# One kernel, three moves: gate products in rows of four, running sums one tile earlier, and a read of x on another queue

## What is computed

```
# block 0: gated linear attention
h = x @ w_in;  q, k, v, z, a = split(h)
g = log_sigmoid(a @ w_a2 + b_a) / 16          # the gates; cumulative sums per chunk of 64
# block 1: indexed sparse attention; after each block: layer norm and a gated side input
# second part: h = rms_norm(x) @ w_in_2, split over five branches
#   A spatial gating, B forgetting attention (big_f = cumsum(log_sigmoid(f))),
#   C mLSTM (b = cumsum(log f); running maximum of i - b), D RWKV-7, M attention to a memory
out = x + concat(branches) * silu(z) @ w_out_2
```

## Time and profile before

| | us |
|---|---|
| median of three runs | 1486.0 (1484.73 to 1486.3) |
| profiled execution, its time | 1486.0 |
| profiled execution, its span | 1484.3 |
| TensorE busy | 1443.8 (97%) |
| VectorE busy | 616.6 (42%) |
| GpSimd busy | 555.9 (37%) |
| ScalarE busy | 526.1 (35%) |

### The profile page before, as it was taken

One profiled execution on the slowest core, in us unless ns is written; L12 is line 12 of the kernel. 1 busy time (PEld: TensorE's weight loads), 2 busy tenths in 40 slices (PEclk: granted clock), 3 DMA queues, 4 the chain that ended last, 5 costly groups with the idle time before them and its releaser, 6 DMA issues.

```text
span 1484.3 us, 25087 instructions
## 1 busy us (share of the span) xinstructions
PE 1443.8 (97%) x10817; PEld 1257.9 (85%) x10817; DVE 616.6 (42%) x1296; ACT 526.1 (35%) x868; POOL 555.9 (37%) x238
## 2 busy tenths in 40 slices
PE   7999999999999999999999999999999999988998
PEld 6888886799999897778788889988997987767897
DVE  6024352123115235379656611344223612487525
ACT  3265223433213332333445521244434322553311
POOL 6333331133332324973374233322434342063221
PEclk9999999999999999999999999999999999998999
DMA  5223321023521323223110043133433222001211
GB/s 175 86 60 99 98 76 39 1 88 104 207 101 58 94 86 113 86 64 107 57 58 30 29 153 115 60 100 114 143 82 95 86 85 86 1 16 59 89 59 57
DMA packets 114668, 122.90 MB, mean 83 GB/s; under 512 B 12665, under 2 KB 107749, under 8 KB 114302
## 3 DMA queue, kind: packets, MB, share of 16 engines
q1 hardware_dynamic: 110864, 113.26, 24.1%
q10 hardware_dynamic: 3694, 8.04, 1.5%
HBM read 114.99 MB, written 6.31 MB: 82 GB/s over the span
## 4 chain that ended last, share of the span: by engine, by line
PE 94%; DVE 2%; ACT 2%; POOL 1%; issue 1%; DMA 0%; SPq 0%; DVEq 0%; ACTq 0%
PE ps L218 89%; PE ps L1462 1%; PE ps L900 1%; PE ps L1468 0%; PE ps L278 0%; ACT xT_high L909 0%; PE ps L3077 0%; PE ps L2278 0%; POOL rk L2814 0%; DMA x_tok<-in_x_dram 0%; DVE xT_low L919 0%; PE ps L2665 0%; PE ps L1038 0%; PE ps L2185 0%; POOL rk L2816 0%
## 5 line engine op out<-in xcount | busy, mean ns | idle before, releaser
L199 POOL TENSOR_TENSOR w_low<-w_ring,w_high 128x2048 fp32r<-128x2048 f32 (+3 forms) x98 | 416.9, 4258 | 707.2 <-ACT w_high L184 671.5
L218 PE MATMUL ps<-w_high,xT_high 128*128 128x256 f32 (+1 forms) x1056 | 303.8, 288 | 6.4 <-POOL w_low L460 4.2
L218 PE MATMUL ps<-w_high,xT_low 128*128 128x256 f32 (+1 forms) x1056 | 296.9, 281 | 0.0
L218 PE MATMUL ps<-w_low,xT_high 128*128 128x256 f32 (+1 forms) x1056 | 296.9, 281 | 0.0
L184 ACT ACTIVATE w_high<-w_ring 128x2048 fp32r<-128x2048 f32 (+1 forms) x91 | 171.5, 1885 | 303.1 <-PE ps L218 302.3
L218 PE MATMUL ps<-xT_high,w_high 128*128 128x512 f32 (+1 forms) x600 | 240.1, 400 | 1.0 <-ACT v_tok L706 0.7
L218 PE MATMUL ps<-xT_high,w_low 128*128 128x512 f32 (+1 forms) x600 | 237.7, 396 | 0.0
L218 PE MATMUL ps<-xT_low,w_high 128*128 128x512 f32 (+1 forms) x600 | 236.7, 394 | 0.0
L218 PEld LDWEIGHTS ps<-w_high,xT_high 128*128 128x128 f32 x1056 | 200.4, 190 | 17.4 <-issue 11.4
L218 PEld LDWEIGHTS ps<-w_low,xT_high 128*128 128x128 f32 x1056 | 200.5, 190 | 2.2 <-issue 2.2
L218 PEld LDWEIGHTS ps<-w_high,xT_low 128*128 128x128 f32 x1056 | 200.3, 190 | 0.0
(11 more groups left out here) (503 smaller groups left out, 2155.9 us busy)
## 6 DMA issues: line engine op xcount, KB each, us to landing
w_ring<-in_gla_w_in_dram SPq DMA_DIRECT2D x24, 1024.0 KB, 5.3
w_ring<-in_dsa_w_in_dram SPq DMA_DIRECT2D x19, 1024.0 KB, 5.2
w_ring<-in_w_in_dram SPq DMA_DIRECT2D x18, 1024.0 KB, 5.2
w_ring<-in_gla_w_out_dram SPq DMA_DIRECT2D x8, 1024.0 KB, 5.1
w_ring<-in_ple_gate_w_dram SPq DMA_DIRECT2D x8, 1024.0 KB, 5.0
w_ring<-in_dsa_w_out_dram SPq DMA_DIRECT2D x8, 1024.0 KB, 4.9
x_scratch<-x SPq DMA_DIRECT2D x4, 1024.0 KB, 6.7
w_ring<-in_w_out_dram SPq DMA_DIRECT2D x4, 768.0 KB, 4.6
```

What stands on the lines that cost most here:

```text
L199: ins = self.nc.gpsimd.tensor_tensor(low[:, part], whole[:, part], high[:, part].bitcast(F32), ALU.subtract)
L218: return self.nc.tensor.matmul(out, lhs, rhs, start=first, stop=last, skip_group_check=not check)
```

## The change

One: the eight gate products of the linear attention are issued in two rows of four, each behind a whole column block (`gates(b)`), instead of one behind each token tile. Two: in the projection the running sums of the log gates are made at one place (behind tile 33) instead of two (behind 33 and 34), and the steps that follow have numbers lower by one; `gates_out` and `mem_turns` keep theirs. Three: the read of x back is issued by SyncE between two of its weight loads instead of by ScalarE behind the U copies, VectorE waits for it ahead of the recurrence instead of ahead of the first addition, and it adds early output tile c in step c instead of in step c + 1.

```diff
--- before.py
+++ after.py
@@ -561,14 +561,14 @@
                         ins = g.split_product(ps[0:GLA_RANK, 4, :], columns(w_a_parts, k), columns(g.xT, k), k == 0, k == KD - 1)
                     ins.then_inc(sem["aT_ready"], add("aT_ready", 1))
 
-                def gate(b, i):
-
-                    if i == 0:
-                        pe.wait_ge(sem["aT_copied"], past["aT_copied"] + 2)
-                    if b:
-                        pe.wait_ge(sem["log_gate"], past["log_gate"] + i + 1)
-                    f = 4 * b + i
-                    g.product(ps[:, 4 + i, :], w_a2[:, f * P:(f + 1) * P], aT[:]).then_inc(sem["u_ready"], add("u_ready", 1))
+                def gates(b):
+
+                    pe.wait_ge(sem["aT_copied"], past["aT_copied"] + 2)
+                    for i in range(4):
+                        if b:
+                            pe.wait_ge(sem["log_gate"], past["log_gate"] + i + 1)
+                        f = 4 * b + i
+                        g.product(ps[:, 4 + i, :], w_a2[:, f * P:(f + 1) * P], aT[:]).then_inc(sem["u_ready"], add("u_ready", 1))
 
                 for c in range(4):
                     for half in range(HALVES):
@@ -593,13 +593,13 @@
                                 ins = g.split_product(ps[:, n % 4, half * CHUNK:(half + 1) * CHUNK], columns(g.xT, k, slice(j * P, (j + 1) * P)),
                                                       columns(w, k), k == 0, k == KD - 1)
                             ins.then_inc(sem[done], add(done, 1))
-                            if c in (1, 2) and half == HALVES - 1:
-                                gate(c - 1, j)
                         g.release(done)
                         if opening:
                             g.turn_tables(pe)
                     if c == 0:
                         low_rank()
+                    elif c < 3:
+                        gates(c - 1)
                 pe.wait_ge(sem["v_copied"], past["v_copied"] + 16)
                 pe.wait_ge(sem["log_gate"], past["log_gate"] + 8)
 
@@ -1849,9 +1849,9 @@
         lg = g.sb(stack, "log_gates", [P, NT, 2 * GH])
         nth_of = {what: nth[i] for i, (_, _, _, _, _, what) in enumerate(tiles)}
         sgu_turns, sgu_masks = 22, 24
-        logs, cums, cum_copies = 30, 33, 35
-        a_turns, a_rows, mu_turns, mu_copies = 36, 37, 38, 39
-        gatings, gate_steps, gated_turns, gates_out = 40, 42, 43, 44
+        logs, cums, cum_copies = 30, 33, 34
+        a_turns, a_rows, mu_turns, mu_copies = 35, 36, 37, 38
+        gatings, gate_steps, gated_turns, gates_out = 39, 41, 42, 44
         mem_turns = 45
         low_tanh = 3 + [what for _, _, _, _, _, what in tiles].index(("small", 0))
         conv_silus = 3 + [what for _, _, _, _, _, what in tiles].index(("kC", 1))
@@ -1907,13 +1907,12 @@
                         for h in range(GH):
                             ins = nc.tensor.transpose(ps[:, 6, h * P:(h + 1) * P], s.w_sgu[:, h, :], g.ident[:])
                         ins.then_inc(sem["w_sgu_turned"], add("w_sgu_turned", 1))
-                    elif i in (cums, cums + 1):
+                    elif i == cums:
                         pe.wait_ge(sem["log_gates"], past["log_gates"] + 1)
-                        for jj in range(NT - 1) if i == cums else (NT - 1,):
+                        for jj in range(NT):
                             for ii in range(jj + 1):
                                 ins = g.product(ps[:, 7, jj * 2 * GH:(jj + 1) * 2 * GH], (g.ones if ii < jj else g.not_before)[:], lg[:, ii, :], ii == 0, ii == jj, check=False)
-                        if i == cums + 1:
-                            ins.then_inc(sem["cum_ready"], add("cum_ready", 1))
+                        ins.then_inc(sem["cum_ready"], add("cum_ready", 1))
                     elif i == a_turns:
                         pe.wait_ge(sem["a_made"], past["a_made"] + 1)
                         for jj in range(NT):
@@ -3300,8 +3299,6 @@
             for j in range(NT):
                 act.wait_ge(sem["U_ready"], past["U_ready"] + j - j % 2 + 2)
                 nc.scalar.activation(U[:, j, :], ps[:, 4 + j // 2, (j % 2) * GW:(j % 2 + 1) * GW], ACT.Copy).then_inc(sem["U_copied"], add("U_copied", 1))
-            act.wait_ge(sem["YT_ready"], past["YT_ready"] + doubled)
-            act.dma_start(x_back, g.x_dram).then_inc(sem["x_back"], add("x_back", 16))
             g.split_high(act, w_out + 3)
 
             def y_squares(j):
@@ -3410,13 +3407,12 @@
             dve.wait_ge(sem["rest_taken"], past["rest_taken"] + 3 * NT)
             for j in range(NT):
                 nc.vector.tensor_tensor(heads(bonus_v[:, j, :]), heads(tok[:, 2, j, :]), bonus[:, j, :].unsqueeze(2).to_broadcast([P, GH, HD]), ALU.mult).then_inc(sem["bonus_v"], add("bonus_v", 1))
+            dve.wait_ge(sem["x_back"], past["x_back"] + 16)
 
             def early_added(u):
 
                 c, j = early_units[u]
                 cols = slice(c * CHUNK, (c + 1) * CHUNK)
-                if u == 0:
-                    dve.wait_ge(sem["x_back"], past["x_back"] + 16)
                 dve.wait_ge(sem["early_ready"], past["early_ready"] + u + 1)
                 nc.vector.tensor_tensor(x_back[:, j, cols], x_back[:, j, cols], ps[:, early_bank(u), 0:CHUNK], ALU.add).then_inc(sem["early_added"], add("early_added", 1))
 
@@ -3437,10 +3433,8 @@
                 for i in range(PAIRS):
                     nc.vector.scalar_tensor_tensor(out=state[:, c + 1, i, :], in0=state[:, c, i, :], scalar=end_decay[:, i, c:c + 1],
                                                                        in1=ps[:, 2 + i, 0:C], op0=ALU.mult, op1=ALU.add).then_inc(sem["state_new"], add("state_new", 1))
-                if c:
-                    early_added(first_early[c - 1])
-
-            early_added(first_early[NCH - 1])
+                early_added(first_early[c])
+
             for j in range(NT):
                 dve.wait_ge(sem["y_sq"], past["y_sq"] + j + 1)
                 sq = y_scratch(j)
@@ -3487,6 +3481,8 @@
         def _(sp):
             sp.wait_ge(sem["mlstm_y_turned"], past["mlstm_y_turned"] + 2)
             g.load_chunks(sp, w_out + RING + 1)
+            sp.wait_ge(sem["YT_ready"], past["YT_ready"] + doubled)
+            sp.dma_start(x_back, g.x_dram).then_inc(sem["x_back"], add("x_back", 16))
             g.load_chunks(sp)
             out_tiles = g.out[0].rearrange("(j p) d -> p j d", p=P)
             for n in range(D // COLS):
```

## The result

The changed kernel takes 1493.55 us (median of 4 runs, 1491.82 to 1495.21), the kernel before 1486.01 us beside it (4 runs, 1484.73 to 1486.3): ratio 1.0053, 95% interval 1.0041 to 1.0065, 7.5 us slower. The prediction said 1485.4 us, in a range of 1483.2 to 1488.5, so the time lies outside the range, on the slow side, to which it gave 0.08. Two executions at a far lower granted clock (one of this kernel, 5005 us, and one of steps_only, 1784 us) are left out of every figure. The profiled execution of the changed kernel took 1492.37 us, with a span of 1490.6 us.

The account below looks back on a forecast made before the run. The prediction took TensorE to bound the kernel, with 94% of the chain. Its terms -2.3 + 1.7 + 0 = -0.6 us gave 1485.4 us from 1486.0, in a range of 1483.2 to 1488.5.

Parts of the forecast that it names:

- What bounds the kernel: Whole kernel: TensorE holds 94% of the chain that ended last, so an edit counts only through TensorE's work or waits.
- First place, the gates (-2.3): Gate products of the linear attention: three of each row of four save 0.39 us of format change, -2.3 us.
- rival A: Gates: each costs 1.25 us also in a row, having its own wait and bank; 1487.7 us, chance 0.10.
- Second place, the steps (+1.7): Running sums and steps one tile earlier: VectorE's scan ends late, TensorE waits 1.7 us for mu_row.
- D: Sums: the scan misses its start before GpSimd's next split, TensorE waits 7.8 us; 1491.5 us, chance 0.04.
- B: Sums: no wait for mu_row, because VectorE is less late than reckoned; 1483.7 us, chance 0.13.
- "0" for the ten products: Running sums: the four products take about 0.82 us behind tile 33 as behind tile 34, so 0.
- Third place, the read of x (0): Read of x on SyncE's queue: lands at 1404.0, just in time for VectorE's recurrence; cost 0, bounds 0 and +3.1 us.
- C: Read of x: the load lands after 1405.4, where the cover ends; 1488.5 us at the chunk rate, chance 0.08.
- VectorE's cover and the additions: Recurrence: TensorE's 1.2 us to spare hides VectorE's wait for the load and additions of 0.33 us per step; 0.
- the list of signs: What the changed profile would show; for the read: SyncE's issue at about 1395.6, landing in under 8 us, no TensorE wait.

Follow-up runs that it names:

- steps_only: Kernel before with only the second part: ten running-sum products at one place and the following steps one tile earlier; 1488.51 us, ratio 1.0017.
- x_act_adds: Kernel before with x read back early on ScalarE's queue, 0.6 us after the last T step, plus VectorE's moved wait and additions; 1485.64 us, ratio 1.0000.
- x_only: Kernel before with only the third part: x read back on SyncE's queue, VectorE's wait and additions moved; 1490.74 us, ratio 1.0035.
- after: The changed kernel, all three parts together, against the kernel before; 1493.55 us, ratio 1.0053.
- gates_only: Kernel before with only the first part: eight gate products in two rows of four; 1487.72 us, ratio 1.0013.
- gate_pairs: Kernel before with the gate products in pairs, behind the second and the fourth token tile; 1485.78 us, ratio 0.9995.
- merge_only: Kernel before with all ten running-sum products behind tile 33, every later step where it stood; 1487.62 us, ratio 1.0009.
- split_sums: Kernel before with the steps one tile earlier but the sums apart, six products behind tile 32, four behind 33; 1490.37 us, ratio 1.0032.
- x_act_same: Kernel before with x read back on ScalarE's queue at the instant SyncE issues it in the changed kernel, VectorE as before; 1490.84 us, ratio 1.0040.
- after_late_read: Changed kernel with SyncE issuing the read of x behind the first WT product, about 1.1 us later; 1490.32 us, ratio 1.0028 against the kernel before.
- pairs_adds: Kernel before with gates in pairs, x read early on ScalarE's queue, and VectorE's additions in their own step; 1485.18 us, ratio 0.9995.

## Why the prediction was wrong, point by point

**What bounds the kernel**: right. Whatever moved the time did so by TensorE.

**First place, the gates (-2.3)**: the saving is right to 0.1 us, rival A is refuted. The sum lacked a term, what the new rows do to TensorE's clock. "What would make the forecast wrong as a whole is a changed pace of TensorE in the stages between, where nothing is edited" came true directly behind the edited places: the rows of four cost +0.7 us in the changed kernel's profile and +1.9 us timed alone.

**Second place, the steps (+1.7)**: VectorE was right throughout, and so was the wait (1.58 us in steps_only); D did not happen (in no profiled execution with the moved steps does a split start before the scan has ended). B looked right in the changed kernel's profile, where no wait is listed, and is not: TensorE came 1.7 us late because of half clock behind the ten products, and so the wait was already paid when it got there. The wait, where it shows, is followed by half clock too. In the changed kernel the place costs 1.7 us, the forecast's size by another way, which is luck; alone it costs +2.7 (3.2 in its rows). "0" for the ten products left out the same term as at the gates: half clock stands behind them in two of four profiled executions, 1.7 us each time. Merged without moving a step they were 1.5 us slower (0.1 to 2.7), which no row shows.

**Third place, the read of x (0)**: here the step failed, "Cost 0". C is refuted, and VectorE's cover and the additions came as worked out (x_act_adds). The load was issued together with the last T step, as the sum had it (not at 1395.6, 0.6 us ahead of it, as the list of signs has it), and took 8.6 us instead of under 8, which the cover of 1.2 us takes up. What I asked was who waits for the load. I did not ask what the load keeps waiting: the 16 KB packets in which TensorE's own instructions arrive over the same DMA engines. One such packet was due 1.6 us behind the very event that now issued the load. It came 3.2 us late, TensorE stood 2.0 us, and half clock followed: 6.8 us of it in the changed kernel's profile (2.9 us of time), 3.4 us in that of x_only. The term is +4.9 us in the changed kernel's rows and +4.9 us timed alone, instead of 0. The rows for it were in the profile before: queue q8 has 85 packets on its page, one of them at 1397.8.

**The sum.** A profiled execution can be followed from place to place by the start of one and the same instruction in it and in the kernel before. The marks are ScalarE's v evictions at 43.2 and 126.30 us (before) for the gates, GpSimd's splits at 1145.1 and 1185.4 us for the sums, and VectorE's last T step at 1396.18 and last state update at 1439.6 us for the read. The table has by how much each kernel gets later between two marks, in us; "elsewhere" is the rest of the difference at the end of the span, from stages that nobody edited.

| kernel | gates | sums | read | elsewhere | together | timed |
|---|---|---|---|---|---|---|
| after | +0.7 | +1.7 | +4.9 | -1.0 | +6.4 | +7.5 |
| gates_only | +1.1 | 0.0 | 0.0 | -0.3 | +0.8 | +1.9 |
| gate_pairs | -1.2 | 0.0 | +0.1 | +1.0 | -0.1 | +0.1 |
| steps_only | 0.0 | +3.2 | 0.0 | +0.1 | +3.3 | +2.7 |
| merge_only | +0.2 | 0.0 | 0.0 | +0.9 | +1.1 | +1.5 |
| split_sums | +0.2 | +3.1 | +0.1 | -1.0 | +2.3 | +4.2 |
| x_only | 0.0 | 0.0 | +3.7 | -0.6 | +3.1 | +4.9 |
| x_act_same | +0.2 | 0.0 | +5.1 | -0.8 | +4.5 | +5.1 |
| after_late_read | +3.0 | +1.6 | +0.1 | +0.3 | +5.0 | +4.2 |
| pairs_adds | -0.8 | 0.0 | +0.1 | +1.6 | +0.9 | -1.0 |

A place that a kernel doesn't touch stays within 0.2 us; the unedited rest moves by 1 us and more from one execution to the next (1.8 us in x_act_adds), so one profile settles where time is lost and not how much in the median. In the changed kernel the forecast's terms -2.3, +1.7 and 0 are +0.7, +1.7 and +4.9: 7.3 us where the sum had -0.6.

The parts timed alone are 1.9 + 2.7 + 4.9 = 9.5 us, the whole 7.5. Half clock behind the sums and the wait for mu_row share the same 1.7 us in the changed kernel, which fits its rows (1.7 us at the sums, 3.2 us in steps_only). But gates and sums together, timed in after_late_read, come to 4.2 us, nearly the 4.6 of the two alone, and most of the missing 2 us would be at the read; the uncertainties are as large, and this was not settled.

**What stays open**: why the clock falls behind one row of gates and not behind the other, and in one execution and not in the next. The Trainium skill (TensorE: Matmul & The Clock Gate, section "What's actually happening") says that the clock follows how busy TensorE has lately been. Behind the wait for mu_row in steps_only and behind the gap at the read, in all three kernels with the gap, the rows agree: TensorE stood, then the clock fell. In split_sums it stood 0.8 and 2.0 us and the clock stayed full. Behind the gates and the sums the rows don't show it: there TensorE's busy time is full in every window before the fall.

## What to carry to other kernels

Before a load is moved, ask not only when it lands and who waits for it, but what else is on the DMA engines in the microseconds behind its issue: the trace lists the packets that bring instructions, and 1 us earlier or later may decide. An engine gap that the profile puts down to "issue" was the sign here. And before small float32 products are gathered into one row, count a half-clock stretch (1.7 us here) against what the row saves: two gates in a row brought none here, four did in some executions.

## What the runs showed of the hardware that I had not expected

- TensorE's instructions came in 16 KB packets during the execution, over the DMA engines that also move the data: 85 packets for 21634 products and weight loads.
- A 2 MB load issued 1.6 us ahead of the moment at which such a packet was due delayed it by 3.1 to 3.4 us and left TensorE without work for 2.0 to 2.3 us; issued 1.0 or 0.5 us ahead of it the load delayed it by at most 0.1 us, and the packet behind it by 1.7 to 2.0 us, which stopped nothing.
- TensorE's clock fell to half behind 3.6 us of products with 17 rows, though TensorE was busy without a break (1.00 in 72 to 74 us, 0.51 in 74 to 76). It does not do so each time: behind the first row of gates_only it stayed full. Behind 1.9 us of them it stayed full in the profiled execution of gate_pairs.
- VectorE's 16 columns took 3.25 to 3.98 us beside GpSimd's split, 0.18 us without it; its copy of 32 columns out of PSUM took 0.18 us beside the same split.
